# Column sums by four 32-column groups, modulation in three accumulated sets, a later group norm and another prefetch order of expert weights, in a two-block transformer kernel

## What is computed

```python
# first block
h = rms_norm(x, g_pre_mix); proj = h @ w_in            # q, k, v of two attentions
o_sb  = stick_breaking_attention(sb_q, sb_k, sb_v)     # 8 heads of 64
o_mla = mla_attention(q_nope, q_rope, k_nope, k_rope, v_mla)
mix = concat([rms_norm(o_sb, g_grp_sb), rms_norm(o_mla, g_grp_mla)]) @ w_o
x = x + rms_norm(mix, g_post_mix)
h = rms_norm(x, g_pre_ffn)
u = causal_depthwise_conv(h @ w_up, conv_w, conv_b); gate, val = split(u)
x = x + rms_norm((gelu(gate) * val) @ w_down, g_post_ffn)
e = p @ w_ple
g = sigmoid(rms_norm(x, g_ple_gate) @ w_ple_gate + b_ple_gate)
x = x + rms_norm(g * e, g_post_ple)

# second block
mod = silu(c) @ mod_w + mod_b                          # (1024) @ (1024 x 6144)
sh1, sc1, g1, sh2, sc2, g2 = split(mod, 6)
h = _rmsnorm(x, norm1_g) * (1 + sc1) + sh1
mix = concat([conv_module, sparse attention, pool_mixer](h @ w_in)) @ w_out
x = x + g1 * mix
h = _rmsnorm(x, norm2_g) * (1 + sc2) + sh2
x = x + g2 * _hier_moe(h, ...)    # 32 experts (1024 x 512, 1024 x 512, 512 x 1024), 2 per token
return _rmsnorm(x, final_g)
```

## Time and profile before

| what | value |
| --- | --- |
| median of 3 runs | 1048.84 us |
| lowest, highest | 1048.14, 1054.28 us |
| profiled execution, its time | 1053.41 us |
| profiled execution, its span | 1051.4 us |
| mean granted TensorE clock | 0.916 |
| PE busy | 852.1 us (81%) |
| DVE, ACT, POOL busy | 315.9, 286.1, 129.1 us |
| bytes moved by DMA | 297.94 MB |
| chain that ended last | PE 57%, DMA 30%, DVE 6%, ACT 4% |

### The profile page before, as it was taken

How to read it: one execution, slowest core, us unless ns; L and a number is a source line. 1 busy time by engine, 2 the same in 40 slices (tenths; PEclk the granted TensorE clock), 3 DMA queues, 4 the chain that set the end, 5 groups by cost and what they waited for, 6 DMA issues and landing times.

```text
span 1051.4 us, 12095 instructions
## 1 busy us (share of the span) xinstructions
PE 852.1 (81%) x5088; PEld 540.2 (51%) x5088; DVE 315.9 (30%) x683; ACT 286.1 (27%) x561; POOL 129.1 (12%) x142
## 2 busy tenths in 40 slices
PE   7999599999998999999979798666666575656555
PEld 6856355799997875477868762212121131212111
DVE  2216432377676441418842300000000010100001
ACT  2325332366565543426352320000000000000001
POOL 0011010144454010016320000000000000000000
PEclk9999899899999999979999899889879787798886
DMA  9932484085443555544425688999999999999993
GB/s 360 401 125 105 171 320 160 10 327 209 178 161 110 205 203 232 177 164 161 158 83 229 251 357 358 428 428 428 428 428 428 428 427 428 428 428 427 428 427 132
DMA packets 22814, 297.94 MB, mean 283 GB/s; under 512 B 2656, under 2 KB 2912, under 8 KB 4704
## 3 DMA queue, kind: packets, MB, share of 16 engines
q1 hardware_dynamic: 22752, 297.09, 69.7%
HBM read 296.03 MB, written 1.05 MB: 283 GB/s over the span
## 4 chain that ended last, share of the span: by engine, by line
PE 57%; DMA 30%; DVE 6%; ACT 4%; POOL 2%; issue 1%; SPq 0%; DVEq 0%; POOLq 0%
PE ps L186 56%; DMA ring<-in_exps 29%; ACT ar L200 2%; DVE ar L206 1%; POOL ar L217 1%; DVE yT L214 1%; ACT yT L200 1%; DVE fr L206 1%; ACT ar L197 1%; DMA ring<-in_win 0%; ACT sq L200 0%; ACT fr L197 0%; DVE misc L575 0%; DVE yT L206 0%; DVE yT L210 0%
## 5 line engine op out<-in xcount | busy, mean ns | idle before, releaser
L186 PE MATMUL ps<-ring,sq 128*32 128x512 f32 x976 | 147.5, 741 | 90.8 <-DMA ring<-in_exps 89.1
L186 PE MATMUL ps<-ring,ar 128*32 128x512 f32 (+1 forms) x712 | 108.5, 695 | 49.4 <-DMA ring<-in_exps 33.4
L186 PEld LDWEIGHTS ps<-ring,sq 128*32 128x32 f32 x976 | 30.4, 123 | 201.6 <-DMA ring<-in_exps 140.5
L186 PE MATMUL ps<-hT,ring 128*128 128x256 f32 (+2 forms) x416 | 96.6, 395 | 6.8 <-DMA ring<-in_win 6.8
L186 PE MATMUL ps<-fr 128*128 128x256 f32 (+1 forms) x660 | 99.3, 305 | 3.1 <-DVE fr L206 3.1
L186 PEld LDWEIGHTS ps<-fr 128*128 128x128 f32 x660 | 89.4, 191 | 9.0 <-DVE fr L206 4.1
L186 PEld LDWEIGHTS ps<-hT,ring 128*128 128x128 f32 (+2 forms) x416 | 80.4, 195 | 20.8 <-DMA ring<-in_win 6.7
L200 ACT ACTIVATE ar<-ps 128x768 f32<-128x768 f32 (+1 forms) x21 | 15.1, 717 | 275.4 <-PE ps L186 270.3
L206 DVE TENSOR_TENSOR ar<-ar,ps 128x512 f32<-128x512 f32 (+1 forms) x10 | 6.4, 641 | 273.1 <-PE ps L186 273.1
L186 PEld LDWEIGHTS ps<-ring,ar 128*32 128x32 f32 (+1 forms) x712 | 26.2, 121 | 111.9 <-issue 57.9
L186 PE MATMUL ps<-ar 128*128 128x512 f32 (+9 forms) x284 | 66.3, 427 | 16.1 <-DVE ar L206 10.9
(11 more groups left out here) (171 smaller groups left out, 986.9 us busy)
## 6 DMA issues: line engine op xcount, KB each, us to landing
ring<-in_exps SPq DMA_DIRECT2D x92, 2048.0 KB, 30.9
ring<-in_modw SPq DMA_DIRECT2D x12, 2048.0 KB, 8.5
ring<-in_wup SPq DMA_DIRECT2D x11, 2048.0 KB, 8.5
...
```

Of the source, the lines that this page charges most:

```text
L186: return pe(lambda e: e.matmul(o, l, r, start=start, stop=stop, skip_group_check=True), *waits, inc=inc)
```

## The change

Six things are edited.

1. `group_sums` sums the squares of up to eight tiles with 32 columns of ones, tile k in the group of output partitions 32 * (k % 4). ACT copies the bank to `sd`. `wide_factor` then adds the groups with one matmul of `ones` (the factor is scaled by 32) where the result is wanted over all partitions, `token_sums` with two one-column matmuls where tokens are wanted on partitions. They take the place of the eight-matmul chain in `x_stats`, the four-matmul chains of both group norms, and the three uses of `x_sums`.
2. The modulation weights are laid out anew: a piece now has 256 rows and 2048 columns, and four pieces make a set. `mod_slot(j)` accumulates over the set in bank 4, with output columns 512 q in group q; only the fourth piece of a set is followed by a DVE copy, and `mod_total` turns the set with four matmuls on four columns of the identity. Pieces 0 to 6 (before: 0 to 5) now lie in the second attention, pieces 0 and 1 both in `mla_fill(0)`, and piece 7 stands where piece 6 was. Nothing stands where piece 7 was.
3. `sb_group` moves from `mla_fill(1)` to `mla_fill(4)`, behind the last pair's Exps on ACT. Its squares are made beside the copies of the attention's output. The second load of the Exp table goes.
4. In the split of h ahead of the feed-forward network, the low part of tile k - 1 follows the multiplication of tile k on DVE.
5. `more` holds pieces 7 to 10; loads are issued in the order 0 to 4, 7 to 10, 5, 6.
6. `gather` is cut in halves with waits of their own; `spread_row` for g2 stays in group 0, `over_tokens` moves to the end of group 1, and the row of `final_g` to the end of group 2.

The diff, cut to its core:

```diff
+
+        def group_sums(b, squares, which):
+
+            nt = len(squares)
+            for k, (x, tok) in enumerate(squares):
+                q = 32 * (k % 4)
+                t = mm(ps[q:q + 32, b, 0:S], ones[:, 0:32], x, k < 4, k >= nt - 4, tok, read[b] if k < 4 else None, d_con,
+                       inc=int(k == nt - 1))
+            return a_copy(sd[:, which, :], bank(b, 0, S), t)
+
+        def wide_factor(b, squares, which, dim, r):
+
+            t = group_sums(b, squares, which)
+            t = mm(bank(b, S, 512), ones, sd[:, which, :], True, True, t, inc=1)
+            read[b] = t = a_fn(sd[:, which, :], bank(b, S, 512), ACT.Sqrt, t, t_eps, bias=eps, scale=1.0 / (32 * dim))
+            return dve(lambda e: e.reciprocal(r, sd[:, which, :]), t)
+
+        def token_sums(b, squares, which):
+
+            t = group_sums(b, squares, which)
+            for j in range(2):
+                t2 = mm(ps[:, b, S + j:S + j + 1], sd[:, which, 128 * j:128 * j + 128], ones[:, 0:1], True, True, t, inc=j)
+            return t2
...
         def x_stats():
-            t = chain(bank(0, 0, S), [(ones, tile(sq, k), tsq[k // 4]) for k in range(8)], d_con)
-            read[0] = t = a_fn(sd[:, 0, :], bank(0, 0, S), ACT.Sqrt, t, t_eps, bias=eps, scale=1.0 / 1024)
-            return dve(lambda e: e.reciprocal(rx0, sd[:, 0, :]), t)
+            return wide_factor(0, [(tile(sq, k), tsq[k // 4]) for k in range(8)], 0, 1024, rx0)
...
         def mod_slot(j):
             w = stream("modw", j)
-            b = 4
-            for k in range(8):
-                q = 32 * (k % 4)
-                t = mm(ps[q:q + 32, b, :], ar[:, cond + 32 * k:cond + 32 * k + 32], w.ap(k * 512, 512), k < 4, k >= 4,
-                       w.ready, t_cond[-1], read[b], inc=int(k == 7))
+            s_, b = j // 4, 4
+            for kk_ in range(2):
+                k = 2 * (j % 4) + kk_
+                for q in range(4):
+                    t = mm(ps[32 * q:32 * q + 32, b, :], ar[:, cond + 32 * k:cond + 32 * k + 32], w.ap(2048 * kk_ + 512 * q, 512),
+                           k == 0, k == 7, w.ready, t_cond[-1], read[b] if k == 0 else None, inc=int(kk_ == 1 and q == 3))
             w.free(t)
-            p = ar[:, modp + 512 * (j % 2):modp + 512 * (j % 2) + 512]
-            read[b] = t = v_copy(p, bank(b), t, part_of.get(j - 2))
-            part_of[j] = t
-            if j not in (0, 8):
-                mod_sum(j - 1)
-
-        def mod_sum(j):
-            p, mb = ar[:, modp + 512 * (j % 2):modp + 512 * (j % 2) + 512], 5
-            for i in range(4):
-                t = mm(ps[:, mb, i:i + 1], p[:, 128 * i:128 * i + 128], ones[:, 0:1], True, True,
-                       part_of[j], read[mb], inc=int(i == 3))
-            part_of[j] = t
-            read[mb] = t = v_tt(mod[:, 4 * j:4 * j + 4], ps[:, mb, 0:4], col("mod_b", 4 * j, 4), ALU.add, t, d_cols)
+            if j % 4 == 3:
+                read[b] = part_of[s_] = v_copy(ar[:, modp:modp + 512], bank(b), t, part_of.get(s_ - 1))
+
+        def mod_total(s_):
+            b = 5
+            for c in range(4):
+                t = mm(ps[:, b, 4 * c:4 * c + 4], ar[:, modp + 128 * c:modp + 128 * c + 128], ident[:, 0:128:32], True, True,
+                       part_of[s_], read[b], inc=int(c == 3))
+            part_of[s_] = t
+            turned_ = ps[:, b, 0:16].rearrange("p (c q) -> p q c", q=4)
+            o, mb = (x.rearrange("p (q c) -> p q c", c=4) for x in (mod[:, 16 * s_:16 * s_ + 16], col("mod_b", 16 * s_, 16)))
+            read[b] = t = v_tt(o, turned_, mb, ALU.add, t, d_cols)
             t_mod.append(t)
...
         def sb_group():
-            r, t_r = norm_scale(oT[:, 0:1024], 4, 512, 0, t_osb, b=5)
-            soft_tables()
+            r = rb[:, 0, :]
+            t_r = wide_factor(5, [(tile(ar, k), t_osb[k // 2]) for k in range(4)], 0, 512, r)
             tg.extend(apply_norm(hT, hT, lambda k: col("g_grp", k), 4, r, t_r))
 
         def mla_fill(i):
-            if i == 1:
+            if i == 0:
+                mod_slot(0)
+                mod_slot(1)
+            elif i < 4:
+                mod_slot(1 + i)
+            elif i == 4:
+                mod_total(0)
                 sb_group()
             else:
-                mod_slot(i - (i > 1))
+                mod_slot(i)
...
-        mod_slot(6)
-        for i in range(4):
-            t = x_sums(i, 2, sqd[i])
-        r, t_r = row_root(2, 1024, 116, t)
+        mod_slot(7)
+        t = token_sums(2, [(tile(sq, k), sqd[k // 2]) for k in range(8)], 0)
+        r, t_r = row_root(2, 32 * 1024, 116, t, S)
         t = over_rows(3, r, t_r, read[3])
         tx = []
-        for k in range(8):
-            th = v_stt(tile(yT, k), tile(xT, k), col("g_pre_ffn", k), bank(3, 0, S), ALU.mult, ALU.mult, t, tt)
-            tx.append(split(tile(yT, k), tile(fr, k, XH), tile(fr, k, XL), v_tt, th))
+        t_hi = []
+        for k in range(9):
+            if k < 8:
+                th = v_stt(tile(yT, k), tile(xT, k), col("g_pre_ffn", k), bank(3, 0, S), ALU.mult, ALU.mult, t, tt)
+                t_hi.append(a_copy(tile(fr, k, XH), tile(yT, k), th))
+            if k:
+                tx.append(v_tt(tile(fr, k - 1, XL), tile(yT, k - 1), tile(fr, k - 1, XH).bitcast(F32), ALU.subtract, t_hi[k - 1]))
         read[3] = th
-        mod_slot(7)
...
             if j == 0:
-                mod_sum(7)
+                mod_total(1)
...
-                for i in range(4):
-                    t = x_sums(i, 3, sqd[i])
-                r3, t_r3 = row_root(3, 1024, 120, t)
+                t = token_sums(3, [(tile(sq, i), sqd[i // 2]) for i in range(8)], 0)
+                r3, t_r3 = row_root(3, 32 * 1024, 120, t, S)
...
         mod_slot(10)
-        for i in range(4):
-            t = x_sums(i, 2, sqd[i])
-        r, t_r = row_root(2, 1024, 124, t)
+        t = token_sums(2, [(tile(sq, k), sqd[k // 2]) for k in range(8)], 0)
+        r, t_r = row_root(2, 32 * 1024, 124, t, S)
...
-        more = {5 + i: (f"more{i}", places, t_arena) for i, places in enumerate(free_at)}
+        more = {7 + i: (f"more{i}", places, t_arena) for i, places in enumerate(free_at)}
...
-        def gather(g):
...
+        def gather(g, n):
+            b = 2 + n
...
+            t_xg[g, n], t_taken[g] = t1, t
+
+        gather(0, 0)
+        gather(0, 1)
+        placed = {j: stream("exps", j, extra=more.get(j)) for j in (0, 1, 2, 3, 4, 7, 8, 9, 10, 5, 6)}
+
+        def expert_slot(j):
+            return placed[j] if j in placed else stream("exps", j)
...
-                    w = stream("exps", j, extra=more.get(j))
+                    w = expert_slot(j)
...
-                                   w.ap(1024 * q + 512 * kk_, 512), k == 0, k == 7, w.ready, t_xg[g], read[hbk],
+                                   w.ap(1024 * q + 512 * kk_, 512), k == 0, k == 7, w.ready, t_xg[g, k // 4], read[hbk],
...
             if g == 0:
-                over_tokens()
-            read[1] = t_av = v_tt(ar[:, av:av + 512], ar[:, sl:sl + 512], W2_, ALU.mult, t, t_sl, p_aT)
-            if g + 1 < NE // 4:
-                gather(g + 1)
+                spread_row(G2ROW, mod[:, 40:48])
+            elif g + 1 < NE // 4:
+                gather(g + 1, 0)
             for k in range(4):
                 t = pe(lambda e, k=k: e.transpose(ps[:, 0, 128 * k:128 * k + 128], ar[:, av + 128 * k:av + 128 * k + 128], ident),
...
-                                     ar[:, ysb + 512 * n:ysb + 512 * n + 512], False, g == NE // 4 - 1, ty[n], t_st, inc=1)
+                                     ar[:, ysb + 512 * n:ysb + 512 * n + 512], g == 0, g == NE // 4 - 1, ty[n], t_st,
+                                     read[YB[2 * j + n]] if g == 0 else None, inc=1)
             p_cmb = t_sum[1, 1]
+            if g == 0:
+                gather(1, 0)
+            if g + 1 < NE // 4:
+                gather(g + 1, 1)
+            if g == 1:
+                over_tokens()
+            if g == 2:
+                spread_row(FROW, col("final_g", 0, 8))
 
 
...
-    A["modw"] = _slots([L["mod_w_2"][:, 512 * i:512 * i + 512] for i in range(12)])
+    A["modw"] = np.stack([_rows(L["mod_w_2"][256 * t:256 * t + 256, 2048 * i:2048 * i + 2048]).reshape(128, SLOT)
+                          for i in range(3) for t in range(4)])
```

78 lines of the change are left out of this document (32 added, 46 removed).

## The result

The changed kernel takes 1019.07 us (median of four runs, 1017.58 to 1026.04) against 1051.56 us before (four runs, 1048.14 to 1055.2): a ratio of 0.9704, 95% interval 0.9642 to 0.9765. The forecast of 1015.5 us lies 3.6 us lower, and the result inside the range. The profiled execution took 1020.2 us (span 1018.4), 33.2 us less than the one of before.

What follows compares the result with a forecast made beforehand. The prediction took the expert weight stream to fix the end, its start set by TensorE and chains between engines before 605 us. Its terms summed to 33.3 us, giving 1015.5 us against the median of 1048.84, range 1006 to 1031.

Steps and rivals of the forecast that it cites:

- The stream's pause: Expert stage: the new load order removes the DMA pause at 632 to 638 us, gain 4.1 us.
- Gate: Gate stage: shorter column sums give 1.6 us, a clock that stays up 1.9 more; 3.5 us taken.
- First norm: `x_stats`: column groups, copy and one matmul replace the eight-matmul chain, gain 1.5 us (1.1 to 1.6).
- Second attention: 93 to 147 us: fewer waits from group norm and modulation copies, gain 8.5 us, less 0.3 for squares.
- Ahead of the feed-forward network: Shorter sums and overlapped split let step 4 start earlier, TensorE deciding; gain 6.6 us (4.5 to 8).
- Ahead of the second block: Shorter sums, no `mod_sum` and less half clock in modulation and projection; gain 7.5 us, between 4.5 and 9.3.
- The 256-column round: Column sums: a round of four 256-column matmuls in separate column groups takes 0.43 us, half the 512-column one.
- groups of 256 columns don't run together: Rival for the column sums: each costs its chain again plus copy and matmul; 1027 to 1032 us, chance 0.07.
- Experts: First expert matmul: no more wait for ACT's half of the gathered tokens, gain 1.65 us.
- The clock falls all the same: Rival: new column sums idle TensorE during ACT's copies, waits replace waits; 22.5 us gained, 1026 us, chance 0.25.
- TensorE becomes the bound: Rival: at half clock among the experts TensorE takes 61.7 us a group against 58.8 of transfers; 1055, chance 0.02.
- The stream does not start earlier: Rival: loads ahead of 605 us are the limit, so only 5.8 us are gained; 1043 us, chance 0.03.

Runs made afterwards that it cites:

- a_col1: The changed kernel with the three square sums (ahead of feed-forward, gate, second block) put back as sixteen one-column matmuls each: 1030.29 us, ratio 0.9782.
- a_again: The changed kernel run again unaltered, for a second trace and more times: 1019.95 us, ratio 0.9704.
- a_norm1: The changed kernel with the group norm put back in step 1 of the second attention: ratio 0.9706.
- b_sets: The kernel before with only the modulation in three accumulated sets, pieces and group norm at their old places: ratio 0.9911.
- a_total5: The changed kernel with the first modulation set's sum moved behind the group norm and the piece of step 5: ratio 0.9717.
- b_order: The kernel before with only the new prefetch order of the expert stream: ratio 0.9962.
- a_split0: The changed kernel with the split ahead of the feed-forward network as before, each tile's product, copy and subtraction in turn: ratio 0.9741.
- a_col128: The changed kernel with the same three square sums put back as sixteen matmuls each, writing 128 equal columns: 1022.14 us, ratio 0.9708.
- b_wide: The kernel before with the matmuls of the three square sums writing 128 equal columns in place of one: ratio 0.998.
- a_router: The changed kernel with 14 matmuls of 256 columns, read by nothing, added behind the router's transposes: ratio 0.97.
- a_warm: The changed kernel with unread matmuls added: seven behind the router's transposes, three behind each piece but the last of the last expert group: 1022.98 us, ratio 0.9703.

## Why the prediction was right, and where not

**What bounds the kernel**: right. The stream runs at some 428 GB/s from 585 us on, its length changes with the prefetch order alone (424.0 to 424.8 or 428.4 to 428.8 us), and a microsecond ahead of the experts moved the end by one: a_col1, 10.0 us later at the first expert matmul than the changed kernel in the traces, ended 10.0 us later. The first expert matmul was forecast 29 us earlier and came 25.5 us earlier.

**The stream's pause**, 4.1: measured 4.0 by the times, and 3.6 to 4.8 by the traces. **Gate**, 3.5: measured 3.05 in all eight traces that have the group sums and the gate's code of the change. The division was right too (1.9 of clock and 1.6; measured 1.69 and 1.36). The size was off by 0.2 us of clock and 0.2 of the sum itself, 2.04 us (396.73 to 398.77) for the 1.86 reckoned. **Group norm of the second attention**, 0.2: nothing; four matmuls took 1.73 us (150.88 to 152.61), and the round, ACT's copy and the matmul behind it take 1.68 (144.49 to 146.17).

**First norm**, 1.5: 1.34 at the norm. It is not what reached the second attention. In six of the ten traces with the new norm, the first one of the changed kernel among them, the clock falls between 76 and 84 us (0.79 in this window, 1.00 in a_again), in none of the four with the old norm, and the last projections ahead of the second attention start at 95.1 to 96.3 us there. The old norm has 94.8 to 95.1, the other four traces with the new one 93.1 to 93.7. What makes the clock fall at that place stays open; the prediction had no term for it.

**The 256-column round**: half of the 512-column one had been taken, 0.43 us, and that is what it takes. One round shows as 0.64 and two as 1.07 us, 0.43 more; the rest is the modelled end of the last matmul. The errors of 0.15 to 0.2 us at each place lie elsewhere: 1.58 us from the sum's start to the first matmul behind the copy (396.73 to 398.31) for 0.86 + 0.65, and 0.46 for the two one-column matmuls for 0.35. The prediction's reading of 1.72 us "from one start to the next work's" was wrong too: that is the pace of pieces in a row, and to other work it is 1.85 us (138.20 to 140.05 in the changed kernel). The rival "groups of 256 columns don't run together" falls with the same rows.

**Second attention**, 8.2 net: 7.14 in the pair of traces; over all traces with the old modulation 52.6 to 56.5 us, with the new one and the new place of the norm 44.7 to 47.8. The size held, but the step that gave two causes did not: "the group norm puts ACT's squares and Sqrt ... ahead of the third pair's mask" is true as a row, and nothing gained by it shows (a_norm1), since the norm waits as long wherever it stands. The other cause, "each `mod_slot` waits for the DVE copy of the last one", carries it all (b_sets), and there is more in later stages. The new wait, forecast at 3.7 us, was 3.91, and its removal gave nothing (a_total5), as another wait of its size stood behind it.

**Ahead of the feed-forward network**, 6.6: 9.1 in the pair, but there the changed kernel had met no half clock. a_again has 19.8 us where the old code has 24.2 and 26.3, so 4.5 to 6.6, and with *ffn*, on which part of the half clock falls, 3.4 to 4.3 us. The argument that TensorE and not VectorE decides at step 4 held: no wait at 187.47 us. The part that was missized is the sum over the rows, 4.3 us: step 1 starts 1.7 us later with it (a_col1 against a_again). Most of the rest had been half clock in one trace: the 32 records took 5.82 us in the trace of before, 3.71 in b_order, with the same code. And the 1.7 us are given back at half clock behind it, so that putting the sum back costs 0.6 us in *pre* and nothing with *ffn*, while the split, put back, costs 2.3 to 4.9 in the traces. That "the removed piece costs nothing here" was not tested alone: a_split0 still lacks the piece, and has *pre* 1.0 us shorter than b_sums, which has it (and the old modulation).

**Ahead of the second block**, 7.5: 7.48 in the pair, by luck. With both old traces and both kinds of new ones the gain lies between 4.1 and 9.1 us. The one-column matmuls have a share in it by the clock: width alone makes 2.8 us in a_col1 against a_col128, and 2.8 or 6.1 in b_wide against the old code.

**Experts**, 1.65: 0.3. The step named the wait for ACT's half, and that wait went; but the gathering ahead of it ran at half clock nearly throughout (granted clock 0.54 from 573.00 to 579.60 us). In the traces without filling it takes 5.2 to 5.4 us in seven and 6.6 to 6.8 in five, whatever was changed ahead; only a_router, where TensorE had 0.96 us of idle time ahead of it, shows 3.81. With 1.6 us of it left, in a_warm, half clock came back within the gathering. These are one trace each, and they speak for a clock that follows the idle time; why it splits the twelve traces as it does stays open.

**The rivals.** "The clock falls all the same" came true in part, and more often than the first trace shows. That trace has it ahead of the second block, right behind the group sums (granted clock 0.57 from 432 to 436 us), and in the gathering, against the sign "a granted clock of 1.0 from the gate's column sums to the second block's first projection". Ahead of the feed-forward network, where the first trace has none, it falls behind the group sums in all five other traces that have them together with the new split. At the gate it falls behind them in none. The gain still stayed well above that rival's 22.5 us. "TensorE becomes the bound" fell: *stream* doesn't change with the half clock among the experts, which every trace has. "The stream does not start earlier" fell with the last piece at 1004.10 us.

**Tail**, "leave alone": 3.4 us in the pair. The change has no part in it; six of the eight other variants of the changed kernel show the short form, 3.71 us for the eight matmuls, and so does b_order with the old code everywhere else.

So the sum of 33.3 us came close to the pair's 33.2 because errors of both signs cancelled. In the pair of traces the forecast was too high by 2.0 us for the stick-breaking attention (the gain of the first norm lost again to the clock), 1.1 for the second attention, 0.9 between the second block's first projection and the router, 1.3 for the experts and some 0.9 for the rest, and too low by 2.5 us ahead of the feed-forward network and 3.4 in the tail. A part of this is luck, then: single terms were off by up to 3.4 us, as much as unchanged code scatters. Against the 31.1 us of the medians the sum was 2.2 us too high.

By the times, undoing one part at a time gives 8.2 (sums over the rows), 3.9 (split), 4.0 (order, done alone), 9.3 (sets, done alone), 1.3 (first norm, by its rows), together 26.7. The other 4.4 us are within the intervals of these, and I can't assign them. Two parts were never tested alone: the removed piece of modulation, and the gathering in halves with `over_tokens` and the rows moved; of the latter the traces show 0.3 us ahead of the experts, and a *stream* at most 0.8 us shorter than that of b_order, which lacks them.
